# Linear attention group restructured: one update product per head, states scanned row by row, outputs beside the scans

## The reference, cut to what matters

```python
def gla_chunked(q, k, v, g, s0):          # chunks of GLA_CHUNK = 16 tokens
    b = jnp.cumsum(g, axis=2); b_last = b[:, :, -1:]
    q_dec = q * jnp.exp(b); k_inv = k * jnp.exp(-b); k_end = k * jnp.exp(b_last - b)
    a = jnp.where(causal, einsum('bnihk,bnjhk->bnhij', q_dec, k_inv), 0.0)
    o_intra = einsum('bnhij,bnjhv->bnihv', a, v)
    def step(s, xs):                       # s: state [head, 32 keys, 64 values]
        qd, ke, vv, dec = xs
        o = einsum('bihk,bhkv->bihv', qd, s)
        return s * dec[..., None] + einsum('bjhk,bjhv->bhkv', ke, vv), o
    ...                                    # o = o_intra + o_inter, backwards the same on flipped tokens
```

## Time and profile before

| what | value |
|---|---|
| median of 3 runs | 4325.37 us (4321.52 to 4325.73) |
| profiled execution | 4329.92 us, its span 4328.1 us |
| TensorE busy | 3532.5 us (82%) |
| VectorE busy | 2639.8 us (61%) |
| ScalarE busy | 2120.1 us (49%) |
| GpSimd busy | 624.3 us (14%) |
| mean granted TensorE clock | 0.899 |
| the four calls of `gla_group` | 2363.5 to 2560.6 and 3639.5 to 3809.1 us of the span, 366.7 us in all |

### The profile page before, as it was taken

One profiled execution on the slowest core, in us unless ns is written; L12 is line 12 of the kernel. 1 busy time (PEld: TensorE's weight loads), 2 busy tenths in 40 slices (PEclk: granted clock), 3 DMA queues, 4 the chain that ended last, 5 costly groups with the idle time before them and its releaser, 6 DMA issues. The chain is left out here.

```text
span 4328.1 us, 51356 instructions
## 1 busy us (share of the span) xinstructions
PE 3532.5 (82%) x17678; PEld 2877.1 (66%) x17678; DVE 2639.8 (61%) x3469; ACT 2120.1 (49%) x2670; POOL 624.3 (14%) x266
## 2 busy tenths in 40 slices
PE   6879999657979999487887767999897886568987
PEld 5767777456767777356786455888675785457865
DVE  3659999745479999684654444444345554444545
ACT  2549998634369999573444013333233443034433
POOL 0005333300024343100020320000000021400000
PEclk9879999879979999798998878999998998689998
DMA  3049999720179999581110001111121110012222
GB/s 100 21 150 416 419 417 410 284 61 11 40 272 419 417 415 409 244 369 49 50 48 1 1 32 38 58 68 58 56 61 49 56 50 1 1 44 98 97 78 78
DMA packets 138104, 643.31 MB, mean 149 GB/s; under 512 B 22002, under 2 KB 33620, under 8 KB 74324
## 3 DMA queue, kind: packets, MB, share of 16 engines
q1 hardware_dynamic: 126484, 620.85, 37.2%
q0 software_dynamic: 10080, 16.80, 1.0%
q10 hardware_dynamic: 1392, 3.74, 0.2%
HBM read 636.82 MB, written 24.41 MB: 153 GB/s over the span
## 5 line engine op out<-in xcount | busy, mean ns | idle before, releaser
L1522 DVE TENSOR_TENSOR w_low<-w_raw,w_high 128x2048 fp32r<-128x2048 f32 x392 | 881.8, 2284 | 65.0 <-ACT w_high L1519 60.6
L1519 ACT CAST w_high<-w_raw 128x2048 fp32r<-128x2048 f32 x392 | 746.3, 1910 | 89.5 <-DMA w_raw<-in_moe_down_dram 39.9
L1829 PE MATMUL banks<-w_high,x_split 128*128 128x512 f32 x1024 | 421.6, 412 | 45.7 <-DVE w_low L1522 38.2
L1829 PE MATMUL banks<-w_low,x_split 128*128 128x512 f32 x1024 | 407.7, 398 | 0.0
L534 PE MATMUL banks<-w_high,x_high 128*128 128x512 f32 (+2 forms) x808 | 310.5, 384 | 70.2 <-DVE w_low L455 45.9
L2873 PE MATMUL banks<-x_high,w_high 128*128 128x512 f32 (+1 forms) x1056 | 320.3, 358 | 36.1 <-DVE w_low L2913 36.1
L422 ACT CAST w_high<-w_raw 128x512 fp32r<-128x512 f32 (+2 forms) x200 | 117.8, 589 | 447.6 <-PE banks L534 418.6
L2873 PE MATMUL banks<-x_high,w_low 128*128 128x512 f32 (+1 forms) x1056 | 323.7, 361 | 0.0
L2873 PE MATMUL banks<-x_low,w_high 128*128 128x512 f32 (+1 forms) x1056 | 319.7, 357 | 0.0
L534 PE MATMUL banks<-w_low,x_high 128*128 128x512 f32 (+2 forms) x808 | 302.9, 375 | 0.0
L534 PE MATMUL banks<-w_high,x_low 128*128 128x512 f32 (+2 forms) x808 | 302.7, 375 | 0.0
(11 more groups left out here) (392 smaller groups left out, 7596.9 us busy)
## 6 DMA issues: line engine op xcount, KB each, us to landing
w_raw<-in_moe_gate_dram SPq DMA_DIRECT2D x132, 1024.0 KB, 10.5
w_raw<-in_moe_up_dram SPq DMA_DIRECT2D x132, 1024.0 KB, 10.2
w_raw<-in_moe_down_dram SPq DMA_DIRECT2D x132, 1024.0 KB, 11.0
w_raw<-in_w_ada_dram SPq DMA_DIRECT2D x48, 1024.0 KB, 10.7
w_raw<-in_ffn_w_up_dram SPq DMA_DIRECT2D x44, 1024.0 KB
w_raw<-in_ffn_w_down_dram SPq DMA_DIRECT2D x88, 256.0 KB, 2.7
w_raw<-in_w_cols_dram SPq DMA_DIRECT2D x48, 256.0 KB, 2.6
w_raw<-in_w_out_dram SPq DMA_DIRECT2D x32, 256.0 KB, 3.0
```

What stands on the lines that cost most here:

```text
L1519: act.copy(ex["WS"][0][:, v % HIGH, :], ex["WR"][:, v % RAW, :]).then_inc(ex["high"], 1)
L1522: dve.tensor_tensor(ex["WS"][1][:, v % LOW, :], ex["WR"][:, v % RAW, :], ex["WS"][0][:, v % HIGH, :].bitcast(F32), ALU.subtract).then_inc( ...
L1829: ins_ = pe.matmul(GU[b][m], stationary(b, kk), WS[w][:, s, k * BANK:(k + 1) * BANK], start=(kk == 0 and w == 0), stop=(kk == KD - 1 and w ...
```

## The change

In each call of `gla_group`:

- `k_end` is laid out by head, both directions side by side, so that one matmul a head gives both directions' updates (64 partitions of a bank). `VX` is a ring of 3 (in the spare rows of `MX`), the banks of the updates a ring of 4. GpSimd spreads two heads of three, VectorE the third.
- The updates leave the banks head by head and direction by direction (32x512): VectorE takes the forward one of each tile's first head, ScalarE the other five of a tile.
- The scores of a tile are computed and masked inside the update loop; `AT` holds all tiles.
- No `DX`: each direction is scanned in 64 instructions, one a value column, 49 elements each, on the decay row itself.
- TensorE multiplies masked scores by v for all tiles ahead of the scans' end, then the forward states after scan 1, then the backward states after scan 2, and turns the rows of tile t-1 after those of tile t. VectorE copies turned rows out at the end. The helper block that turned the rows is gone.
- `QB` is one buffer for both groups, cleared once beside the first group's transposes. GpSimd fills the forward half inside its spreading loop, ScalarE the backward half after the updates.

```diff
@@ decays
-                            ins_ = dve.tensor_tensor(KE[:, t, d, :], E[:, b, 2, c], UG[:, t, QK:2 * QK], ALU.mult)
+                            ins_ = dve.tensor_tensor(KE[:, t, :, d, :], *(x.rearrange("p (h k) -> p h k", h=GLA_H) for x in (
+                                E[:, b, 2, c], UG[:, t, QK:2 * QK])), ALU.mult)
@@ gla_group
-            DX = self.sbuf(ctx, "decay_wide", [W3, GLA_DV, SL])
-            self.transpose(name + "T", groups)
+            def clear_blocks(pool, done):
+                pool.memset(QB[:, :, :, :, :], 0.0).then_inc(done, 1)
+                pool.wait_ge(done, 1)
+            self.transpose(name + "T", groups, clear_blocks if grp == 0 else None)
+            VR, UR, SR = 3, 4, 4
+            by_dve = lambda n, d: d == 0 and n % 3 == 0
+            from_pool = lambda n: n % 3 != 2
+            def place(copy, n, d):
+                t, hh = n // HG, n % HG
+                s0 = slot(d, t * NC8) + 1
+                r = slice(hh * GLA_DK, (hh + 1) * GLA_DK)
+                dst = ST[r, 0, :, s0:s0 + NC8] if d == 0 else ST[r, 1, :, s0 - NC8 + 1:s0 + 1][:, :, ::-1]
+                return copy(dst, UB(n)[d * GLA_DK:(d + 1) * GLA_DK].rearrange("p (c v) -> p v c", v=GLA_DV))
@@ GpSimd
+                    for t in range(NTT):
+                        for n in range(t * HG, (t + 1) * HG):
+                            if from_pool(n):
+                                expand(pool, n)
+                        if t % 2 == 1:
+                            pool.wait_ge(expanded[0], expands((t + 1) * HG - 2))
+                            block_q(pool.tensor_copy, 0, t // 2).then_inc(blocked, 1)
+                            pool.wait_ge(blocked, t // 2 + 1)
@@ TensorE
+                    for n in range(N):
+                        pe.wait_ge(expanded[0 if from_pool(n) else 1], expands(n))
+                        if n >= UR:
+                            pe.wait_ge(up_out_v, evacs(n - UR, True))
+                            pe.wait_ge(up_out_a, evacs(n - UR, False))
+                        pe.matmul(UB(n), KE[:, n // HG, grp * HG + n % HG].rearrange("p d k -> p (d k)"),
+                                  VX[:, n % VR].rearrange("p c v -> p (c v)"), start=True, stop=True).then_inc(updates, 1)
+                        if n % HG == HG - 1 and n // HG < upd:
+                            scores(n // HG)
...
+                    pe.wait_ge(masked, upd * HG)
+                    for t in range(upd):
+                        for hh in range(HG):
+                            for d in range(2):
+                                pe.matmul(OB(t)[:, hh, :], V(t, hh), AT[:, t, hh, d, :],
+                                          start=(hh == 0 and d == 0), stop=False, skip_group_check=True)
+                    pe.wait_ge(blocked, HG)
...
+                    pe.wait_ge(scanned, 1)
+                    for t in range(upd):
+                        inter(t, 0)
+                    pe.wait_ge(scanned, 2)
+                    pe.wait_ge(blocked_back, HG)
+                    for t in range(upd):
+                        inter(t, 1).then_inc(mixed, 1)
+                        if t >= 1:
+                            turn_rows(t - 1)
+                    turn_rows(upd - 1)
@@ VectorE
+                    for n in range(N):
+                        if by_dve(n, 0):
+                            dve.wait_ge(updates, n + 1)
+                            place(dve.tensor_copy, n, 0).then_inc(up_out_v, 1)
+                        if n % 3 == 2:
+                            if n + 3 < N:
+                                expand(dve, n + 3)
+                            t = n // HG
+                            for i in range(t * HG, (t + 1) * HG if t < upd else t * HG):
+                                dve.wait_ge(scored, i + 1)
+                                dve.tensor_tensor(AT[:, t, i % HG], SB(i).rearrange("p (d n) -> p d n", d=2), masks,
+                                                  ALU.mult).then_inc(masked, 1)
...
+                    for d in range(2):
+                        for v in range(GLA_DV):
+                            ins_ = dve.tensor_tensor_scan(ST[:, d, v, :], DEC[:, d, grp, :], ST[:, d, v, :], 0.0,
+                                                          ALU.mult, ALU.add)
+                        ins_.then_inc(scanned, 1)
...
+                    for t in range(upd):
+                        dve.wait_ge(turned, t + 1)
+                        dve.tensor_copy(ON[:, t, grp * W:(grp + 1) * W], RB(t)).then_inc(rows_done, 1)
@@ ScalarE
+                    for n in range(N):
+                        act.wait_ge(updates, n + 1)
+                        for d in range(2):
+                            if not by_dve(n, d):
+                                place(act.copy, n, d).then_inc(up_out_a, 1)
+                    for hh in range(HG):
+                        block_q(act.copy, 1, hh).then_inc(blocked_back, 1)
+                    for t in range(upd):
+                        act.wait_ge(mixed, t + 1)
+                        if t >= 2:
+                            act.wait_ge(turned, t - 1)
+                        act.copy(OT[:, t % 2], OB(t)).then_inc(out_done, 1)
```

More of the change, by code:

```diff
@@ L2436, in mixer_layer @@
                 ON = self.sbuf(ctx, "gla_rows", [P, upd, GV])
-                self.gated_linear(layer, UG, UR, LR, ON, upd)
+                self.gated_linear(layer, UG, UR, LR, MX, ON, upd)
                 G, loads = self.gate_rows(ctx, layer, 2, 1 if last else 2)
@@ L2488, in gated_linear @@
             with ExitStack() as ctx:
-                KE = self.sbuf(ctx, "k_end", [P, NTT, 2, QK])
+                KE = self.sbuf(ctx, "k_end", [P, NTT, GLA_H, 2, GLA_DK])
                 QD = self.sbuf(ctx, "q_dec", [P, NTT, 2, QK])
@@ L2502, in gated_linear @@
                     self.decays(layer, UG, G, QD, KI, KE, DEC, slot, SL)
+                QB = self.sbuf(ctx, "q_blocks", [HG * GLA_DK, 2, upd * NC8, HG, CHUNK])
                 for grp in range(2):
-                    self.gla_group(layer, grp, UG, QD, KI, KE, DEC, ON, upd, slot, SL)
+                    self.gla_group(layer, grp, UG, QD, KI, KE, DEC, MX, ON, QB, upd, slot, SL)
             self.gla_output(layer, ON, UR, upd)
@@ L2591, in decays, with gla_group @@
             self.end(sem)
-    def gla_group(self, layer, grp, UG, QD, KI, KE, DEC, ON, upd, slot, SL):
+    def gla_group(self, layer, grp, UG, QD, KI, KE, DEC, MX, ON, QB, upd, slot, SL):
         nc = self.nc
-        NC8, W3 = P // CHUNK, HG * GLA_DK
+        NC8, W3, N = P // CHUNK, HG * GLA_DK, NTT * HG
+        VR, UR, SR = 3, 4, 4
         cols = slice(grp * W3, (grp + 1) * W3)
@@ L2754, in gla_group @@
-            W = HG * GLA_DV
-            self.transpose(name + "oT", [([OT[:, hh, t * P:(t + 1) * P] for hh in range(HG)],
-                                          ON[:, t, grp * W:(grp + 1) * W], None, None) for t in range(upd)])
+            (updates, up_out_v, up_out_a, zeroed, blocked, scanned, scored, masked, mixed, out_done, turned, rows_done) = (
+                sem(n) for n in ("updates", "up_out_v", "up_out_a", "zeroed", "blocked", "scanned", "scored", "masked",
+                                 "mixed", "out_done", "turned", "rows_done"))
@@ new lines, in gla_group @@
+            OB = lambda t: self.ps[0:GLA_DV, t, 0:HG * P].rearrange("p (h n) -> p h n", h=HG)
+            RB = lambda t: self.ps[:, 6 + t % 2, 0:HG * GLA_DV]
+            masks = self.consts[:, self.const_at["upto"][0]:self.const_at["upto"][0] + 2 * P].rearrange(
+                "p (d n) -> p d n", d=2)
+            ident = self.const("ident")
+            by_dve = lambda n, d: d == 0 and n % 3 == 0
+            evacs = lambda n, dve: sum(1 for m in range(n + 1) for d in range(2) if by_dve(m, d) == dve)
@@ new lines, in gla_group, with expand @@
+            from_pool = lambda n: n % 3 != 2
+            expands = lambda n: sum(1 for m in range(n + 1) if from_pool(m) == from_pool(n))
+            def expand(eng, n):
+                if n >= VR:
+                    eng.wait_ge(updates, n - VR + 1)
+                eng.tensor_tensor(VX[:, n % VR], V(n // HG, n % HG).unsqueeze(1).broadcast_to([P, NC8, GLA_DV]),
+                                  self.const("chunk").unsqueeze(2).broadcast_to([P, NC8, GLA_DV]),
+                                  ALU.mult).then_inc(expanded[0 if from_pool(n) else 1], 1)
@@ L2758, in gla_output @@
+            self.end(sem)
     def gla_output(self, layer, ON, UR, upd):
```

177 lines of the change are left out of this document (51 added, 126 removed).

## The result

The changed kernel takes 4207.26 us (median of 4 runs, 4203.09 to 4212.22) where the kernel before takes 4325.18 (median of 4): 0.973 of it, 95% interval 0.9713 to 0.9746. That is 118 us less; forecast were 106. The profiled execution, one of these four, took 4212.2 us (4329.9 before).

A forecast was written before the change was run, and what follows sets the result against it. Stages on different engines stand behind one another, VectorE filling the scans and TensorE the outputs, with no DMA to hide them. 23.9 - 15.6 + 97.8 = 106.1 us saved gives 4219 us; whole range 4200 to 4270.

The forecast's parts named there:

- signs of being wrong: Scans starting over 0.2 us apart, long ScalarE or VectorE waits for TensorE in the updates, or forward products ending after scan two.
- part 3: Outputs behind the scans: 15.5 us a call in the first layer, 11.1 in the second, a gain of 97.8 us.
- Part 1: Update stage of the four calls: TensorE sets a pace of 3.5 us a tile, a gain of 23.9 us.
- Part 2: Scans: 128 short instructions a call at 0.174 us each, 22.3 us a call, 15.6 us lost.
- the ends: Price of a short scan: 0.27 us if each waits for the one before, 0.17 if they follow closely.
- The rival of the full fixed part: Scans: each short scan pays the full fixed part, 0.27 us, 48.6 us more, total 4268; chance 0.13.
- Coupled updates: Update loop: each tile waits for GpSimd's copy or VectorE's maskings, stage stays 29 to 31 us, total 4243; chance 0.13.
- the lanes that the prediction itself gave: Update loop, us a tile: TensorE 3.5 with handover, ScalarE 3.1, VectorE 2.8, GpSimd 2.4 to 3.2.
- No overlap: Outputs: a whole call's products wait for both scans, so 37 us and masked products come back, total 4286; chance 0.03.
- Slower: Scans: restarting the feedback 512 times; gain gone at 0.38 us a scan, 4360 at 0.45; chance 0.03.
- The edits at nothing: Clearing `QB`, ScalarE's block copies and `k_end` in runs of 32 cost nothing; GpSimd's last copy might cost under 2 us.

## Why the prediction was right or wrong

**The direction and the bound** were right. Stages on different engines stood behind one another with no transfer to hide them, and what came off them reached the end; 118 us against 106, 4207 in a range of 4200 to 4270. That the sum came so close is in part luck. The scans cost 11.6 us less than forecast, the updates gained 2.4 us less and the outputs 3.4 less: errors of both signs that leave 5.8. The other 5.8 lie outside the stages. Of its own signs of being wrong one came true: in the first layer the forward products end after the second scan (part 3 below).

**Part 1, updates:** 23.5, 24.8, 24.1, 24.1 forecast, 24.2, 24.7, 24.7, 25.3 measured; the pace of 3.5 us a tile was 3.38 by TensorE's products. The size was right, and so was TensorE as the lane that counts. The first call of this execution had a start at half clock too (its stretch shows 0.93): its first tile's six records took 4.39 us and not 2.79, which is more than its 0.7 us. In the fourth call they took 5.38, 2.6 us more than at the full clock, where I had 1.3. As a cause, "with three buffers it no longer waits out the spreading" holds only in part: with the two directions side by side two buffers do nearly as well. The third buffer is one of two remedies, each enough by itself, and the prediction did not see the other.

**Part 2, scans:** this is the mis-sized term, 22.3 us a call forecast, 19.4 measured, 11.6 us over the four calls, which is more than the whole error of the sum in the calls (5.8). The choice between the ends was right (they follow closely, 0.151 us apart against the 0.234 of a record). Both its parts were too high: I took 0.109 us for the elements, where 49 x 2.08 is 0.102, and 0.065 fixed, where it is 0.049. The 2.22 ns of the long scan holds its start and end and, likely, the GpSimd copies beside it: at 2.08 ns a scan of 3136 would last 6.7 us with the 0.08 by which a record is longer than the distance, and it lasted 6.97 to 7.19. That the copies stretch scans is shown for short ones; for the long ones it was not tried. The sizes fit: the long scans were over 6.65 us by 0.5 in the first layer and 0.3 in the second, where a copy held short scans up by 0.6 and 0.4.

**The rival of the full fixed part** (0.27 us a scan, 4268) is out: the distance is 0.151. The Trainium skill (VectorE: DVE Perf Modes, The DRAIN you can't avoid), which the prediction quoted for the next operation waiting until the pipe is empty, adds in the same paragraph that a next operation that is not held starts earlier; the prediction left that out, and these scans, started before the one in front has ended, are such a case. What the Trainium skill (Vector Engine (DVE) Microarchitecture Reference, Measured stream behaviour on trn2) puts on an instruction, about 75 ns, was 49 here.

**Part 3, outputs:** 15.5 and 11.1 us forecast behind the scans, 17.2 and 11.0 to 11.2 measured. The step that failed is "the forward half of the states' products ... under the second scan of 11.1". It fitted by 0.1 us only because the scans were priced too long. TensorE's forward half (10.9 us) does not fit in a second scan of 9.7, and ends 1.4 us late. What was won in part 2 was so given back in part, in the first layer. The other 0.3 us are two small errors: a tile took 2.46 us in place of 1.83 + 0.36 = 2.19, in four tiles, as the first two have nothing to turn between them; and the end of the stage was shorter than the 2.7 us forecast. In the second layer, where the forward half has room, these cancel.

**The other rivals.** Coupled updates (4243) did not happen; the lanes that the prediction itself gave, 3.5, 3.1, 2.8 and 2.4 to 3.2 us a tile, were not within 10% of each other as its rival says. No overlap: I priced it at 67 us above the forecast; made to happen, it cost 64 to 68. That agreement is in part luck, as the price had masked products of 30 us at the full clock; they are 27 there, and the lower clock adds 10. Slower at over 0.38 us a scan: more than twice what was measured. The edits at nothing stayed near it: GpSimd's last block copy ended before the scans; the second call's transposes, which follow the outputs, took 6.3 us for 5.5 at a granted clock of 0.60 for 0.73.

## What to carry to other kernels

Price a run of short independent instructions by the distance from start to start, which a row of three neighbours gives, and not by the duration of one. When stages on different engines stand behind one another, put them side by side before making any of them faster; then look again which engine is last, since here eight columns a scan gained 5.2 us a call where VectorE was the bound and 2 where TensorE was. A double buffer can be too small when its reader streams it twice, one pass after the other: let the products that share it run side by side, or add a buffer, and don't pay for both. Look at the granted clock before choosing what to put beside a long stage of another engine: here the masked products gained by it and the products of the states did not.

## What the runs showed of the hardware

- A scan on VectorE (fp32, 96 partitions) costs 49 ns and 2.08 ns an element of distance, from 49 to 392 elements (0.151, 0.457, 0.865 us).
- GpSimd's copies and VectorE's scans look as if they exclude each other instruction by instruction: beside a long scan a copy lasted up to 7.11 us; beside short ones 0.60 to 0.88, and each copy held the scans up by some 0.6 us (768 columns) or 0.4 (512). That is argued from durations; no row shows the mechanism.
- fp32 products of 32 columns into different partitions stream side by side also when they are two instructions and when they go to two banks (12 records in 2.77 us in one bank, 6 of 64 columns in 2.79; 3.46 us a tile with two banks, where the same partitions gave 4.47). The Trainium skill (TensorEngine Tiling (Array Packing), Key Properties) says that tiles operate independently; the runs agree.
- The products of the states (48 columns on 96 partitions, with 64 columns of weights each) took the same time at both levels of the clock: 32 records in 3.66 us at a granted clock of 1.00, 75 in 8.10 us at 0.50, both 0.11 us a record. The masked products of a tile (128 columns) took 1.52 us at 1.00 and 2.82 at 0.50.
